# Two 2 MB loads of expert weights become one 4 MB load for gate and up

## The reference

```python
def moe_expert_choice(h, router_w, w_gate, w_up, w_down):
    B_, T, _ = h.shape
    cap = CAPACITY_FACTOR * T // N_EXPERTS
    aff = jax.nn.softmax((h @ router_w).astype(jnp.float32), axis=-1)
    gate, idx = lax.top_k(jnp.swapaxes(aff, 1, 2), cap)
    bidx = jnp.arange(B_)[:, None, None]
    xs = h[bidx, idx]
    hid = jax.nn.silu(jnp.einsum('becd,edf->becf', xs, w_gate)) * jnp.einsum('becd,edf->becf', xs, w_up)
    ye = jnp.einsum('becf,efd->becd', hid, w_down) * gate[..., None].astype(h.dtype)
    return jnp.zeros_like(h).at[bidx, idx].add(ye)
```

## Time and profile before

| | |
|---|---|
| time, median of 3 runs | 1550.55 us (1549.97 to 1551.77) |
| time of the profiled execution | 1551.3 us |
| its span, first to last instruction | 1549.5 us |
| PE busy | 1207.3 us (78%) |
| DVE busy | 562.5 us (36%) |
| ACT busy | 423.9 us (27%) |
| moved by DMA | 520.90 MB in 118719 packets, mean 336 GB/s |
| mean granted TensorE clock | 0.89 |

### The profile page before, as it was taken

How to read it: one execution, slowest core, us unless ns; L and a number is a source line. 1 busy time by engine, 2 the same in 40 slices (tenths; PEclk the granted TensorE clock), 3 DMA queues, 4 the chain that set the end, 5 groups by cost and what they waited for, 6 DMA issues and landing times.

```text
span 1549.5 us, 18615 instructions
## 1 busy us (share of the span) xinstructions
PE 1207.3 (78%) x8122; PEld 730.7 (47%) x8122; DVE 562.5 (36%) x829; ACT 423.9 (27%) x553; POOL 29.9 (2%) x36
## 2 busy tenths in 40 slices
PE   4999999999656656656666656656666899999998
PEld 1878899943111212111111111211211589999997
DVE  3887776511101101101101101101101497777566
ACT  2865646232000000000000000000000454467545
POOL 0012000000000000000000000000000000000000
PEclk9999999999778878778867888878778999999999
DMA  9546859699999999999999999999999855555551
GB/s 364 207 156 229 301 209 337 223 403 429 426 428 428 428 428 427 428 428 426 428 428 427 427 428 428 427 427 429 428 427 428 327 164 163 163 183 184 184 186 55
DMA packets 118719, 520.90 MB, mean 336 GB/s; under 512 B 7264, under 2 KB 85088, under 8 KB 90736
## 3 DMA queue, kind: packets, MB, share of 16 engines
q1 hardware_dynamic: 118496, 519.64, 83.9%
q10 hardware_dynamic: 144, 0.09, 0.0%
HBM read 518.66 MB, written 1.05 MB: 335 GB/s over the span
## 4 chain that ended last, share of the span: by engine, by line
DMA 53%; PE 43%; DVE 2%; ACT 1%; SPq 1%; issue 0%; DVEq 0%
DMA pair<-in_wu 27%; PE B L1697 16%; DMA pair<-in_wd 12%; DMA pair<-in_wg 11%; PE B L1705 6%; PE B L2113 4%; PE B L1709 3%; DMA wslot<-in_w_in 2%; PE B L1824 2%; PE B L2147 1%; PE B L1675 1%; PE B L1812 1%; PE B L1827 1%; DMA wslot<-in_w_out 1%; DMA wslot<-in_ada_w 1%; PE B L2074 0%
## 5 line engine op out<-in xcount | busy, mean ns | idle before, releaser
L2113 PE MATMUL B<-pair,xs 128*32 128x512 f32 x2048 | 323.1, 758 | 193.0 <-DMA pair<-in_wu 121.5
L2113 PEld LDWEIGHTS B<-pair,xs 128*32 128x32 f32 x2048 | 63.2, 124 | 413.0 <-issue 180.1
L2147 PE MATMUL B<-pair,hidT 128*32 128x512 f32 x1008 | 167.9, 799 | 102.1 <-DMA pair<-in_wd 96.6
L1697 PE MATMUL B<-hnh,whj 128*128 128x256 f32 x488 | 138.1, 283 | 0.0
L1697 PE MATMUL B<-hnh,wslot_r 128*128 128x256 f32 x488 | 137.6, 282 | 0.0
L1697 PE MATMUL B<-hn_r,whj 128*128 128x256 f32 x488 | 137.1, 281 | 0.0
L2147 PEld LDWEIGHTS B<-pair,hidT 128*32 128x32 f32 x1008 | 32.3, 128 | 218.6 <-DMA pair<-in_wd 143.2
L955 DVE TENSOR_TENSOR wslot_r<-wslot,whj 128x2048 fp32r<-128x2048 f32 x52 | 118.9, 2289 | 31.3 <-ACT whj L509 31.3
L509 ACT ACTIVATE whj<-wslot 128x2048 fp32r<-128x2048 f32 x51 | 97.2, 1913 | 87.6 <-PE B L1697 82.0
L1289 DVE SCALAR_TENSOR_TENSOR x<-B,mod,x 128x256 f32<-128x256 f32 x128 | 56.0, 480 | 163.5 <-PE B L2092 163.3
L1320 DVE COPY ye<-B 128x512 f32<-128x512 f32 x15 | 10.4, 692 | 269.6 <-PE B L2147 269.6
(11 more groups left out here) (505 smaller groups left out, 1908.8 us busy)
## 6 DMA issues: line engine op xcount, KB each, us to landing
pair<-in_wg SPq DMA_DIRECT2D x64, 2048.0 KB, 41.2
pair<-in_wu SPq DMA_DIRECT2D x64, 2048.0 KB, 40.9
pair<-in_wd SPq DMA_DIRECT2D x62, 2048.0 KB, 40.9
wslot<-in_w_in SPq DMA_DIRECT2D x58, 1024.0 KB, 5.2
aslot<-in_ada_w SPq DMA_DIRECT2D x20, 1024.0 KB, 7.2
wslot<-in_ada_w SPq DMA_DIRECT2D x4, 1024.0 KB, 9.1
wslot<-in_w_out SPq DMA_DIRECT2D x4, 1024.0 KB, 8.5
wslot<-in_wa SPq DMA_DIRECT2D x4, 1024.0 KB, 5.1
```

The source lines that it names most:

```text
L1697: mm = e.matmul(ps, w[:, k, :], x(k), start=k == 0 and j == 0, stop=k == kn - 1 and j == 2)
L2113: mm = e.matmul(B[b][32 * j:32 * j + 32, :], XS[x // 8][:, k, 32 * (x % 8):32 * (x % 8) + 32], tile_at_page(t)[:, 512 * j:512 * j + 512], ...
L2147: mm = e.matmul(B[3 + db][32 * r:32 * r + 32, :], hidT[:, 128 * c + 32 * j:128 * c + 32 * j + 32], v2(tile_at_page(t + c // 2))[:, c % 2, ...
```

## The change

The weights of gate and up are loaded four tiles at a time. A partition p then holds rows 4p to 4p + 3 of a block of 512 rows, one run of 32 KB. From tile 28 on there are four homes of four pages: slots 0 to 3, zone pages 8 to 11, 0 to 3 and 4 to 7, in this order. A down load stays a pair and takes half of a home. The first 14 loads (tiles 0 to 27) keep their pairs and their homes, but their gate and up pairs are now halves of the 32 KB runs, 16 KB each. Zone page 12 is no longer a home. A load waits for the last tile of all loads that overlap its pages. The features stand four apart, in the gathers and in the transposition of the scale and shift, which has 16 matmuls for 4. `WH2[2]` and `c2` change pages (0 for 6), and waits at the end of the experts follow the new homes. The diff, without lines that only rename:

```diff
-        WH2 = [put(f"whj{i}", 2048, page(p), FR) for i, p in enumerate((14, 15, 6))]
+        WH2 = [put(f"whj{i}", 2048, page(p), FR) for i, p in enumerate((14, 15, 0))]
...
-        c2, c2l = both("c2", 2048, page(0))
+        c2, c2l = both("c2", 2048, page(6))
...
-        zpair = lambda i: BASE + i
-        TURN = [zpair(2), zpair(4), zpair(12), zpair(0), zpair(6), 0, 2, zpair(8), zpair(10)]
+        zone_at = lambda i: BASE + i
         EXTRA = BASE + MORE + AUX
         APART = EXTRA + 1
-        PAIRS = TURN[:2] + [EXTRA] + TURN[3:] + [APART] + 2 * (TURN[:2] + TURN[3:])
-        PAIRS += [TURN[i % 9] for i in range(12 * NE - len(PAIRS))]
-        tile_page = lambda t: PAIRS[t // 2]
-        pairs = {r: put(f"pair{r}", 2 * SLOT, page(17) if r == EXTRA else slots_at + r * SLOT if r < BASE else page(r - BASE)) for r in set(PAIRS) - {APART}}
+        LOADS = [(2 * i, 2, r) for i, r in enumerate((zone_at(2), zone_at(4), EXTRA, zone_at(0), zone_at(6), 0, 2, zone_at(8), zone_at(10), APART,
+                                                      zone_at(2), zone_at(4), zone_at(0), zone_at(6)))]
+        for t in range(28, 24 * NE, 4):
+            r = zone_at(8) if t == 24 * NE - 4 else (0, zone_at(8), zone_at(0), zone_at(4))[(t - 28) // 4 % 4]
+            LOADS += [(t, 2, r), (t + 2, 2, r + 2)] if t % 24 >= 16 else [(t, 4, r)]
+        load_of = {t: load for load in LOADS for t in range(load[0], load[0] + load[1])}
+        tile_page = lambda t: load_of[t][2]
+        homes = {(n, r): put(("pair" if n == 2 else "four") + str(r), n * SLOT, page(17) if r == EXTRA else slots_at + r * SLOT if r < BASE else page(r - BASE))
+                 for _, n, r in LOADS if r != APART}
         apart = (slots[4], put("apart", SLOT, page(15)))
 
         def tile_at_page(t):
-            return apart[t % 2] if tile_page(t) == APART else pairs[tile_page(t)][:, t % 2 * SLOT:t % 2 * SLOT + SLOT]
-
-        last_tile = lambda r: max(2 * i + 1 for i in range(12 * NE) if PAIRS[i] == r)
-
-        def before(t):
-
-            earlier = [i for i in range(t // 2) if PAIRS[i] == PAIRS[t // 2]]
-            return 2 * earlier[-1] + 1 if earlier else None
-
-        def expert_src(t):
+            t0, n, r = load_of[t]
+            return apart[t - t0] if r == APART else homes[n, r][:, (t - t0) * SLOT:(t - t0 + 1) * SLOT]
+
+        in_slot = lambda s, load: load[2] <= s < load[2] + load[1]
+
+        def last_tile(s):
+
+            return max(load[0] + load[1] - 1 for load in LOADS if in_slot(s, load))
+
+        def before(load):
+
+            t0, n, r = load
+            earlier = [x[0] + x[1] - 1 for x in LOADS if x[0] < t0 and any(in_slot(s, x) for s in range(r, r + n))]
+            return max(earlier) if earlier else None
+
+        def expert_src(t, n):
             e_, m, k = t // 24, t % 24 // 8, t % 8
             if m == 2:
                 return a["wd"][e_, 256 * k:256 * k + 512, :].rearrange("(p c) n -> p (c n)", c=4)
-            return a["wu" if m else "wg"][e_, 128 * k:128 * k + 256, :].rearrange("(p c) n -> p (c n)", c=2)
+            rows = a["wu" if m else "wg"][e_, 512 * (k // 4):512 * (k // 4) + 512, :].rearrange("(p c) n -> p (c n)", c=4)
+            return rows[:, k % 4 * SLOT:(k % 4 + n) * SLOT]
...
-                e.dma_start(pairs[tile_page(t)], expert_src(t)).then_inc(*landed[tile_page(t)]("expert", t))
+                e.dma_start(homes[n, r], expert_src(t, n)).then_inc(*landed[r]("expert", t))
...
-            for t in range(10, 24 * NE, 2):
+            for load in LOADS[5:]:
+                t = load[0]
                 if t == 10:
 
                     e.wait_ge(*p_proj.at("b", 1, 1))
...
                     e.wait_ge(*p_proj.at("tile", SECOND - BASE + t - 9))
                 elif t == 14:
                     e.wait_ge(*p_proj.at("wo", 3))
-                elif before(t) is not None:
-                    e.wait_ge(*p_exp.at("tile", before(t)))
-                elif tile_page(t) == zpair(12):
-                    e.wait_ge(*a_moe.at("xs", 1, 7))
+                elif before(load) is not None:
+                    e.wait_ge(*p_exp.at("tile", before(load)))
...
-                    e.wait_ge(*p_exp.at("tile", last_tile(tile_slot(n) // 2 * 2)))
+                    e.wait_ge(*p_exp.at("tile", last_tile(tile_slot(n))))
                 elif n == SECOND + 4:
-                    e.wait_ge(*p_exp.at("tile", max(i for i in range(24 * NE) if tile_page(i) == APART)))
+                    e.wait_ge(*p_exp.at("tile", last_tile(APART)))
                 else:
                     e.wait_ge(*p_proj.at("tile", n - BASE))
                 weights(n)
                 if n == SECOND + BASE - 1:
-                    e.wait_ge(*p_exp.at("tile", last_tile(zpair(10))))
+                    e.wait_ge(*p_exp.at("tile", last_tile(zone_at(11))))
...
-            e.wait_ge(*p_exp.at("tile", last_tile(zpair(0))))
+            e.wait_ge(*p_exp.at("tile", last_tile(zone_at(1))))
...
-            for b_ in range(2):
-                for hf in range(2):
-                    mm = e.matmul(B[4][64 * hf:64 * hf + 64, 0:16].rearrange("p (m q b) -> p b m q", m=2, b=2)[:, b_], ident[:, b_::2],
-                                  ffs.rearrange("p (m q h) -> p h m q", m=2, h=2)[:, hf], start=True, stop=True)
+            for b_ in range(4):
+                for hf in range(4):
+                    mm = e.matmul(B[4][32 * hf:32 * hf + 32, 0:16].rearrange("p (m q b) -> p b m q", m=2, b=4)[:, b_], ident[:, b_::4],
+                                  ffs.rearrange("p (m q h) -> p h m q", m=2, h=4)[:, hf], start=True, stop=True)
...
-                    mm = e.matmul(B[b][:, 0:32], H2k[:, i, 256 * (k // 2) + k % 2:256 * (k // 2) + 256:2], Pm[:, i, 0, :], start=i == 0, stop=i == 1)
+                    mm = e.matmul(B[b][:, 0:32], H2k[:, i, 512 * (k // 4) + k % 4:512 * (k // 4) + 512:4], Pm[:, i, 0, :], start=i == 0, stop=i == 1)
...
-                    if k % 2 == 0:
+                    if t == load_of[t][0]:
```

More of the change, by code:

```diff
@@ L420, in experts @@
             def experts(t):
-                if tile_page(t) == APART:
-                    e.dma_start(apart[0], expert_src(t)[:, 0:SLOT]).then_inc(*landed[APART]())
-                    e.dma_start(apart[1], expert_src(t)[:, SLOT:2 * SLOT]).then_inc(*landed[APART]("expert", t))
+                n, r = load_of[t][1:]
+                if r == APART:
+                    e.dma_start(apart[0], expert_src(t, 2)[:, 0:SLOT]).then_inc(*landed[APART]())
+                    e.dma_start(apart[1], expert_src(t, 2)[:, SLOT:2 * SLOT]).then_inc(*landed[APART]("expert", t))
                     return
                 if t == 24 * NE - 2:
-                    e.dma_start(pairs[tile_page(t)][:, 0:SLOT], expert_src(t)[:, 0:SLOT]).then_inc(*l_last())
-                    e.dma_start(pairs[tile_page(t)][:, SLOT:2 * SLOT], expert_src(t)[:, SLOT:2 * SLOT]).then_inc(*landed[tile_page(t)]("expert", t + 1))
+                    e.dma_start(homes[n, r][:, 0:SLOT], expert_src(t, 2)[:, 0:SLOT]).then_inc(*l_last())
+                    e.dma_start(homes[n, r][:, SLOT:2 * SLOT], expert_src(t, 2)[:, SLOT:2 * SLOT]).then_inc(*landed[r]("expert", t + 1))
                     return
-                e.dma_start(pairs[tile_page(t)], expert_src(t)).then_inc(*landed[tile_page(t)]("expert", t))
+                e.dma_start(homes[n, r], expert_src(t, n)).then_inc(*landed[r]("expert", t))
             def later(j):
@@ L720, in scalar @@
                 if k == 7:
-                    e.wait_ge(*p_exp.at("tile", 2 * PAIRS.index(EXTRA) + 1))
+                    e.wait_ge(*p_exp.at("tile", last_tile(EXTRA)))
                     pp_left(0)
@@ L2073, in gather @@
                 for i in range(2):
-                    mm = e.matmul(B[b][:, 0:256 - c0], H2k[:, i, 256 * (k // 2) + k % 2:256 * (k // 2) + 256:2], Pm[:, i, 8 * hf + c0 // 32:8 * hf + 8, :], start=i == 0, stop=i == 1)
+                    mm = e.matmul(B[b][:, 0:256 - c0], H2k[:, i, 512 * (k // 4) + k % 4:512 * (k // 4) + 512:4], Pm[:, i, 8 * hf + c0 // 32:8 * hf + 8, :], start=i == 0, stop=i == 1)
                 mm.then_inc(*p_misc("gather", hf, k))
```

## The result

The changed kernel takes 1562.55 us (median of 4 runs, 1559.6 to 1563.44) against 1551.12 us; the ratio is 1.0071, with a 95% interval of 1.0054 to 1.0089. The forecast was 1548.1 with a range up to 1554.2. The profiled execution took 1563.44 us, its span is 1561.6.

What follows compares the result with a forecast made beforehand. The prediction took the experts' weight stream at 428 GB/s to bound the kernel, with PE waiting beside it. Longer packets -4.8 and a hole +2.4 gave -2.4 us: 1548.1 from the median of 1550.55, range 1543.1 to 1554.2.

Steps and rivals of the forecast that it cites:

- part 2: Start of the stream, queue thin: the load of tiles 28 to 31 waits for tile 13, leaving a hole, +2.4 us.
- Part 5: Small edits (larger transposition, gathers with stride 4, swapped pages): no new wait on the path, cost 0, uncovered +1.23 us.
- Part 1: Experts' weight stream: 59 loads of 4 MB with 32 KB packets save nine packets each at 9.0 ns, -4.8 us.
- C: Rival: long packets cost what two short ones do, so only the hole stays, 1553.0 us; chance 0.17.
- D: Rival: partitions 32 KB apart in memory read slower than 16 KB apart, 1555.9 us; chance 0.10.
- F: Rival: each load pays its own fixed time, so 59 loads fewer give -165 us, 1385 us; chance 0.01.
- the sum: Landing estimate for tiles 28 to 31: issue at 341.11 plus 10.3 plus 4.9 for the second half, 356.3 us.
- the prediction's own line: Hole size against lead before the forerunner's landing, through 3.6 us with 2.0 and 4.6 us with 0.6.
- Part 3: Steady stage: sixteen slots freed four tiles at a time; at worst 12 us late leaves 17 us queued, cost nothing.
- Part 4: End of the experts: PE starts the last gate/up load 4.9 us later but catches up in down, cost 0.
- rival E: PE is late at the end because its clock stays at the lower level from 1200 us, +3, 1551.1 us; chance 0.08.
- A: Likeliest case, the summed forecast of 1548.1 us, own range 1546 to 1551; chance 0.49.

Runs made afterwards that it cites:

- e2: The kernel before with one wait more: the load of tiles 18 and 19 waits for PE's tile 5; 1561.17 us, ratio 1.0057.
- e8: The changed kernel, its wait for tile 5 kept, with H2k written in gather order (stride 1); 1558.3 us, ratio 1.0047.
- e4: The changed kernel without the wait for tile 5 and with H2k written in gather order (stride 1); 1547.91 us, ratio 0.9974.
- e3: The kernel before with only the new feature order (stride 4, 16 KB halves of 32 KB runs) and the larger transposition; 1554.53 us, ratio 1.0025.
- e1: The changed kernel with APART renumbered, so the load of tiles 18 and 19 no longer waits for tile 5; 1553.45 us, ratio 1.0010.
- e6: e4 with each 4 MB load issued as two 2 MB loads into the same home; 1552.41 us, ratio 1.0012.

## Why the prediction was wrong

**What failed first: "The load before them was issued at 304.29" (part 2), taken over to the changed kernel.** The front of the change was costed with the old waits, although `before` had been rewritten. Part 5 put new waits at nothing ("no new wait on the path: 0") but had only the gathers and the swapped pages in view, and part 2 looked for holes only from tile 28 on. The new wait stands on the path, while the queue is thin. Working out the new `before` for each of the first 14 loads would have shown tile 5 against the load of tiles 18 and 19. What the runs put in its place: +9.9 us alone (e2), +10.4 in the new homes (e8 over e4). No rival of the prediction had it.

**"Gathers with stride 4 for 2 ...: same instructions, ...: 0" (part 5) failed.** Same number, not the same duration: 325 ns for 196 ns a weight load. In expert 0 PE sets the releases of tiles 0 to 13 and the queue is thin, so the 0.5 us more of each group of four gathers reaches the end: +3.2 us (e3), 5.5 (e1 over e4), 4.2 (the changed kernel over e8, with the half-rate clock in it).

**Part 1 was right.** -4.8 us forecast, -4.5 measured (e4 below e6), 430 GB/s forecast and measured. Rivals C (no gain from long packets) and D (slower pitch) are excluded by e6 and e3, F by the small gain itself.

**Part 2's hole came at its size in e4, partly by luck.** It measured 2.4 us there, but the load took 14.2 us to land where the sum had 15.2, and its forerunner landed 1.0 earlier than in the sum: two misses that cancel. By the prediction's own line the lead of 2.1 us before that landing would have made some 4 us. In the changed kernel the hole is absent: the loads piled up behind the stall, so that tile 26 was issued at 339.90 and took 21.0 us, the four at 348.72 took 21.9, and they land 9.7 apart:

```profile
pair<-in_wg SPq DMA_DIRECT2D x1, 2048.0 KB, 21.0
...
four<-in_wg SPq DMA_DIRECT2D x1, 4096.0 KB, 21.9
```

A wait for DMA did appear in front of tile 28 there, 0.8 us, one of the signs that the prediction named: the stall had made all landings late.

**Part 3 held** in the changed kernel: behind the stall the DMA share is 0.97 or more in each 5 us up to 380. In e1, without the stall but with slow gathers, it is not: 315 GB/s from 345 to 350 us, and a hole of 1.3 us in front of tile 32, where part 2 expected none. **Part 4 held**: PE catches up by the second pair of down. The changed kernel's last expert, to be read against the earlier trace rows:

```profile
1212.73 5.23 PE L2124 MATMUL B<-four,xs 128*32 128x512 f32 x32 [4.70 <-DMA four<-in_wu]
...
1220.29 1.92 PE L2158 MATMUL B<-pair,hidT 128*32 128x512 f32 x16 [0.69 <-ACT hidT L747]
1222.52 1.92 PE L2158 MATMUL B<-pair,hidT 128*32 128x512 f32 x16 [0.31 <-DMA pair<-in_wd]
...
1227.48 1.92 PE L2158 MATMUL B<-pair,hidT 128*32 128x512 f32 x16 [1.95 <-DMA pair<-in_wd]
...
1232.46 1.07 PE L2158 MATMUL B<-pair,hidT 128*32 128x512 f32 x8 [0.97 <-DMA pair<-in_wd]
```

The second, third and last waits are for the DMA again, not for PE (rival E did not come). The larger transposition takes 0.66 us, where the earlier trace rows has 0.41.

**The chances** do not add up in one place: a third of A's 0.49 is 0.16, not 0.21, so "faster" should have been 0.32 and not 0.37.

**The account.** A chain of kernels, each against its neighbour: from the kernel before to new homes and order with dense gathers and 2 MB loads +1.7 (e6), loads of 4 MB -4.5 (e4), the stall +10.4 (e8), slow gathers and whatever goes with them +4.2. The four add up to the whole by construction, +11.8 against 1550.73 (+11.4 against the 1551.12 of the result's own runs), so the sum proves nothing; what bears them is that each step after the first changes one thing, that the stall was also measured by itself, and that the landings of tile 383 in the table give the four steps as +0.4, -3.9, +10.3 and +5.2, within 1.3 us. Nearly all of the gain that part 1 expected did arrive; it was given back three times over before 350 us.

## What to carry to other kernels

When a function that derives waits is rewritten, list its result for every load, not only for those that are meant to change; numbers given to places that are no real neighbours (`EXTRA + 1`) turn into overlaps once ranges are compared. A queue that covers everything in the steady stage covers little while it is thin: there one late issue stops all loads behind it, and each PE instruction ahead of a release counts. An operand's stride is part of its cost: write data once in the order in which they are read many times.

## What the runs showed of the hardware

A load of 128 float32 columns as stationary operand takes 191, 196, 259, 325 and 330 ns at strides of 1, 2, 3, 4 and 8 elements. Going from packets of 16 KB to 32 KB saves 7.8 to 8.5 ns for each packet fewer (e4 against e6, by landings and by medians), close to the 9.0 ns of the line from 1 to 16 KB. Partitions 16 KB or 32 KB apart in memory both stream at 428 GB/s. A stall costs nearly the time that it leaves the queue dry, less the holes that the loads behind it fill: 10.0 us dry cost 9.9 (e2), 12.3 cost 10.4 (e8 over e4), and 17.0 put the landing of tile 47 16.5 us late (the changed kernel).
